# Four sums of squares in a two-block transformer kernel, regrouped between VectorE and TensorE

## The reference

```
# block 1
h = rmsnorm(x, attn_pre_g)                        # norm n0
mix = concat(nsa_attention, swa_attention) @ w_o
x = x + rmsnorm(mix, attn_post_g)                 # norm y1 -> x1
h = rmsnorm(x, mlp_pre_g)                         # norm x1
a, u = split(h @ w_gate_up)
y = (gelu(causal_dwconv(a)) * u) @ w_down
x = x + rmsnorm(y, mlp_post_g)                    # norm y2 -> x2
x = x + (p @ w_ple) * sigmoid(x @ w_ple_gate)     # -> x3
# block 2
h = rms_norm(x, norm_mix)                         # norm x3
x = x + concat(neighbourhood, retention) @ w_out  # -> x4
h = rms_norm(x, norm_mlp)                         # norm x4
x = x + square(relu(h @ w_up)) @ w_down           # -> x5
return rms_norm(x, norm_final)                    # norm x5

def rmsnorm(x, g): return x * rsqrt(mean(x * x, axis=-1) + 1e-6) * g
```

## Time and profile before

| | us |
|---|---|
| median of 3 runs | 1358.34 (1356.01 to 1365.15) |
| the profiled execution | 1356.79 |
| its span, first to last instruction | 1355.0 |

### The profile page before, as it was taken

One profiled execution on the slowest core, in us unless ns is written; L12 is line 12 of the kernel. 1 busy time (PEld: TensorE's weight loads), 2 busy tenths in 40 slices (PEclk: granted clock), 3 DMA queues, 4 the chain that ended last, 5 costly groups with the idle time before them and its releaser, 6 DMA issues.

```text
span 1355.0 us, 16819 instructions
## 1 busy us (share of the span) xinstructions
PE 1309.6 (97%) x6196; PEld 1086.0 (80%) x6196; DVE 808.7 (60%) x1562; ACT 640.3 (47%) x1234; POOL 149.8 (11%) x133
## 2 busy tenths in 40 slices
PE   8999999989999999999989999999999999999996
PEld 7897888878888888888767867788878888888885
DVE  5779989565664556445567877578553333344343
ACT  6777666454444444234344654576453233242342
POOL 0012111000110011001001100022221011020110
PEclk9989999989999999999979999999999999999998
DMA  7211010322232332323322221332223233232321
GB/s 259 83 40 47 32 32 24 131 70 78 94 93 86 109 101 86 102 93 101 93 63 78 84 74 53 93 125 90 76 73 114 94 94 101 86 108 94 95 78 62
DMA packets 63008, 118.20 MB, mean 87 GB/s; under 512 B 7632, under 2 KB 9040, under 8 KB 62672
## 3 DMA queue, kind: packets, MB, share of 16 engines
q1 hardware_dynamic: 61776, 113.48, 26.4%
q10 hardware_dynamic: 1152, 3.67, 0.8%
HBM read 115.02 MB, written 2.10 MB: 86 GB/s over the span
## 4 chain that ended last, share of the span: by engine, by line
PE 80%; DVE 12%; ACT 5%; issue 3%; DMA 1%; SPq 0%; POOL 0%; DVEq 0%; ACTq 0%
PE bank L529 23%; PE bank L531 23%; PE bank L530 23%; PE bank L586 1%; PE bank L588 1%; PE bank L587 1%; DVE pp L1866 1%; PE bank L698 1%; PE bank L615 1%; DVE wl L1695 1%; DVE ptl L1889 1%; DVE pp L1883 1%; ACT wh L1099 1%; PE bank L684 1%; PE bank L685 1%
## 5 line engine op out<-in xcount | busy, mean ns | idle before, releaser
L1695 DVE TENSOR_TENSOR wl<-raw,wh 128x512 fp32r<-128x512 f32 (+1 forms) x356 | 269.5, 772 | 362.7 <-ACT wh L1099 361.7
L1099 ACT ACTIVATE wh<-raw 128x512 fp32r<-128x512 f32 (+1 forms) x394 | 239.8, 623 | 299.0 <-PE bank L531 287.0
L529 PE MATMUL bank<-AH,wh 128*128 128x512 f32 x840 | 333.1, 397 | 8.8 <-DVE AL L1709 3.7
L531 PE MATMUL bank<-AH,wl 128*128 128x512 f32 x840 | 331.8, 395 | 0.0
L530 PE MATMUL bank<-AL,wh 128*128 128x512 f32 x840 | 329.7, 392 | 0.0
L529 PE MATMUL bank<-BH,wh 128*128 128x512 f32 x624 | 248.8, 399 | 5.8 <-DVE wl L1695 3.7
L531 PE MATMUL bank<-BH,wl 128*128 128x512 f32 x624 | 246.6, 395 | 0.0
L530 PE MATMUL bank<-BL,wh 128*128 128x512 f32 x624 | 245.1, 393 | 0.0
L529 PEld LDWEIGHTS bank<-AH,wh 128*128 128x128 f32 x840 | 158.9, 189 | 45.8 <-issue 5.4
L530 PEld LDWEIGHTS bank<-AL,wh 128*128 128x128 f32 x840 | 158.8, 189 | 35.2 <-issue 0.2
L531 PEld LDWEIGHTS bank<-AH,wl 128*128 128x128 f32 x840 | 158.8, 189 | 34.9
(11 more groups left out here) (286 smaller groups left out, 1672.1 us busy)
## 6 DMA issues: line engine op xcount, KB each, us to landing
raw<-in_w_dn SPq DMA_DIRECT2D x108, 256.0 KB, 2.6
raw<-in_w_gu SPq DMA_DIRECT2D x88, 256.0 KB, 2.6
raw<-in_w_up SPq DMA_DIRECT2D x64, 256.0 KB, 2.6
raw<-in_w_nsa SPq DMA_DIRECT2D x16, 256.0 KB, 2.6
raw<-in_w_pg SPq DMA_DIRECT2D x16, 256.0 KB, 2.6
raw<-in_w_naq SPq DMA_DIRECT2D x16, 256.0 KB, 2.7
nbi<-in_na_bias ACTq DMA_DIRECT2D x8, 448.0 KB, 3.5
raw<-in_w_swa SPq DMA_DIRECT2D x10, 256.0 KB, 2.7
```

The costliest lines, as they stand in the source:

```text
L529: t.matmul(o, w, xh, start=start, stop=False, skip_group_check=skip)
L531: return t.matmul(o, wl, xh, start=False, stop=stop, skip_group_check=skip)
L1099: a.activation(W[i % NW].h[:, 0:n], RAW[i % NRAW][:, 0:n], ACT.Copy).then_inc(*s_wh.up(i))
L1695: v.tensor_tensor(w.l[:, 0:n], RAW[i % NRAW][:, 0:n], w.h[:, 0:n], ALU.subtract).then_inc(*s_wl.up(i))
```

## The change

- y1, y2, x5: VectorE adds the squares of the chunks 1 to 6, each behind the addition of the next result chunk. TensorE sums only the added tile and that of chunk 7: two groups of four matmuls in place of five.
- x1: the square of chunk 0 goes to `r2_bc`, VectorE adds those of the chunks 1 to 7, and TensorE does one group of four, behind the first gate/up product, in place of eight groups.
- Each of these matmuls has 64 columns of ones in place of one, so a block's sum stands 64 times in the bank, and the first of each 64 is read.
- ScalarE takes the root from PSUM with the mean's factor and eps inside the instruction; before its wait it does a root of one column (`warm`), whose result nothing reads. VectorE's instruction for the mean is gone; the Newton step is rearranged, with four instructions behind the root in both kernels.
- The back product is four matmuls of 128 columns, each behind its own diagonal tile.
- In the first gate/up product the 12 matmuls of chunk 0 are ordered so that the eight that need only `AH` come first (`fresh`).
- The last half of the last product is done one result chunk at a time (`G=1, kpp=4`, with the weights packed to suit), and the loading and splitting of the last pieces is placed between the steps of the norm.

```diff
+                    if fresh is not None and s == 0:
+                        x = src[ks[0]]
+                        e.wait_ge(s_xh.at((fresh, ks[0])))
+                        for g in range(G):
+                            t.matmul(bs[g][:, :], w.h[:, g * P:g * P + P], x.h, start=True, stop=False)
+                        for g in range(G):
+                            t.matmul(bs[g][:, :], w.l[:, g * P:g * P + P], x.h, start=False, stop=False)
+                        e.wait_ge(ready(ks[0]))
+                        for g in range(G):
+                            m = t.matmul(bs[g][:, :], w.h[:, g * P:g * P + P], x.l, start=False, stop=False)
+                        m.then_inc(*s_mm.up(("p", i)))
+                        continue
...
-            def squares_of(key, c, src, first, last):
+            def squares_of(key, src, first, last, *done):
 
                 b = bank.ap(("st", key))
                 for i in range(4):
-                    m = t.matmul(b[:, i:i + 1], src[:, P * i:P * i + P], ones[:, 0:1], start=first and i == 0, stop=last and i == 3, skip_group_check=True)
-                m.then_inc(*s_st.up((key, "c", c), *([key] if last else [])))
-
-            def soon(key):
+                    m = t.matmul(b[:, 64 * i:64 * i + 64], src[:, P * i:P * i + P], ones[:, 0:64], start=first and i == 0, stop=last and i == 3,
+                                 skip_group_check=True)
+                m.then_inc(*s_st.up(*done, *([key] if last else [])))
+
+            def soon(key, alone=True):
 
                 b, free = bank.take(("st", key))
-                e.wait_ge(*free, s_ad.at((key, 3)))
-                squares_of(key, 3, r2_bc, True, False)
-                for c in range(4, 8):
-                    e.wait_ge(s_sq.at((key, c)))
-                    squares_of(key, c, sqr.ap((key, c)), False, c == 7)
+                e.wait_ge(*free, s_ad.at((key, 6 if alone else 7)))
+                squares_of(key, r2_bc, True, not alone)
+                if alone:
+                    e.wait_ge(s_sq.at((key, 7)))
+                    squares_of(key, sqr.ap((key, 7)), False, True, (key, "c", 7))
                 bank.give(("st", key))
 
             def soon_back(key):
                 b, free = bank.take(("bk", key))
-                e.wait_ge(*free, s_rs.at((key, "diag")))
-                t.matmul(b[:, :], ones[:, :], tmp.ap((key, "d"))[:, 0:T], start=True, stop=True).then_inc(*s_st.up(("bk", key)))
+                e.wait_ge(*free)
+                for i in range(4):
+                    c = slice(P * i, P * i + P)
+                    e.wait_ge(s_rs.at((key, "diag", i)))
+                    m = t.matmul(b[:, c], ones[:, :], tmp.ap((key, "d"))[:, c], start=True, stop=True)
+                m.then_inc(*s_st.up(("bk", key)))
...
-            def x1_squares(c):
-                if c == 0:
-                    b, free = bank.take(("st", "x1"))
-                    e.wait_ge(*free)
-                e.wait_ge(s_sq.at(("x1", c)))
-                squares_of("x1", c, sqr.ap(("x1", c)), c == 0, c == 7)
-                if c == 7:
-                    bank.give(("st", "x1"))
-
             c0, g0 = 0, 0
             for gi, n in enumerate(FF1):
                 for c in range(c0, c0 + n, 2):
                     keys = [("a", c), ("u", c), ("a", c + 1), ("u", c + 1)]
-                    between = None
-                    if c == 0:
-                        between = {k: lambda k=k: x1_squares(k - 1) for k in range(1, 8)}
-                    elif c == 2:
-                        x1_squares(7)
+                    if c == 2:
+                        soon("x1", False)
                         embedded(2)
                         soon_back("x1")
-                    product("w_gu", g0, A, x1, range(8), 4, 1, keys, between)
+                    product("w_gu", g0, A, x1, range(8), 4, 1, keys, fresh="x1" if c == 0 else None)
...
+                    if gi == 3 and i:
+                        for g in range(4):
+                            product("w_dn2", 56 + 2 * g, A, up_ready, range(8), 1, 4, [keys[g]])
+                            bank.give(keys[g])
+                        continue
...
-                e.wait_ge(s_rs.at((key, "var")))
-                a.activation(rv[:, 4:8], rv[:, 0:4], ACT.Sqrt).then_inc(*s_fn.up((key, "sqrt")))
+                b = bank.ap(("st", key))[:, 0:256].rearrange("p (b q) -> p b q", q=64)[:, :, 0]
+                a.activation(warm[key], eps, ACT.Sqrt)
+                e.wait_ge(s_st.at(key))
+                a.activation(rv[:, 4:8], b, ACT.Sqrt, bias=eps, scale=1.0 / 1024).then_inc(*s_fn.up((key, "sqrt")))
...
-                b = bank.ap(("st", key))
-                e.wait_ge(s_st.at(key))
-                v.tensor_scalar(rv[:, 0:4], b[:, 0:4], 1.0 / 1024, EPS, ALU.mult, ALU.add).then_inc(*s_rs.up((key, "var")))
-                bank.read(("st", key), (s_rs, (key, "var")))
+                b = bank.ap(("st", key))[:, 0:256].rearrange("p (b q) -> p b q", q=64)[:, :, 0]
+                g, h = rv[:, 4:8], rv[:, 0:4]
                 e.wait_ge(s_fn.at((key, "sqrt")))
-                v.reciprocal(rv[:, 4:8], rv[:, 4:8]).then_inc(*s_rs.up((key, 1)))
+                v.reciprocal(g, g).then_inc(*s_rs.up((key, 0)))
+                e.wait_ge(s_rs.at((key, 0)))
+                v.scalar_tensor_tensor(out=h, in0=b, scalar=1024 * EPS, in1=g, op0=ALU.add, op1=ALU.mult).then_inc(*s_rs.up((key, 1)))
+                bank.read(("st", key), (s_rs, (key, 1)))
                 e.wait_ge(s_rs.at((key, 1)))
-                v.scalar_tensor_tensor(out=rv[:, 0:4], in0=rv[:, 0:4], scalar=-0.5, in1=rv[:, 4:8], op0=ALU.mult,
-                                       op1=ALU.mult).then_inc(*s_rs.up((key, 2)))
+                v.scalar_tensor_tensor(out=h, in0=h, scalar=-0.5 / 1024, in1=g, op0=ALU.mult, op1=ALU.mult).then_inc(*s_rs.up((key, 2)))
                 e.wait_ge(s_rs.at((key, 2)))
-                v.tensor_tensor(rv[:, 0:4], rv[:, 0:4], rv[:, 4:8], ALU.mult).then_inc(*s_rs.up((key, 3)))
-                e.wait_ge(s_rs.at((key, 3)))
-                v.scalar_tensor_tensor(out=rv_out, in0=rv[:, 0:4], scalar=1.5, in1=rv[:, 4:8], op0=ALU.add,
-                                       op1=ALU.mult).then_inc(*s_rs.up((key, 4)))
+                v.scalar_tensor_tensor(out=rv_out, in0=h, scalar=1.5, in1=g, op0=ALU.add, op1=ALU.mult).then_inc(*s_rs.up((key, 4)))
                 d = tmp.ap((key, "d"))
                 e.wait_ge(s_rs.at((key, 4)), *tmp.before((key, "d")), s_tab.at("tab"))
                 for i in range(4):
-                    m = v.tensor_scalar(d[:, P * i:P * i + P], ident[:, :], rv_out[:, i:i + 1], None, ALU.mult)
-                m.then_inc(*s_rs.up((key, "diag")))
+                    v.tensor_scalar(d[:, P * i:P * i + P], ident[:, :], rv_out[:, i:i + 1], None,
+                                    ALU.mult).then_inc(*s_rs.up((key, "diag", i)))
                 tmp.read((key, "d"), (s_st, ("bk", key)))
...
-            def add_square(key, c, dst):
-                if 0 < c < 4:
+            def add_square(key, c):
+
+                if c:
                     e.wait_ge(s_sq.at((key, c)), s_sq.at((key, 0)), *([s_ad.at((key, c - 1))] if c > 1 else []))
-                    v.tensor_tensor(dst[:, :], dst[:, :], sqr.ap((key, c))[:, 0:T], ALU.add).then_inc(*s_ad.up((key, c)))
+                    v.tensor_tensor(r2_bc[:, :], r2_bc[:, :], sqr.ap((key, c))[:, 0:T], ALU.add).then_inc(*s_ad.up((key, c)))
...
+                    add_square("x1", c - 1)
+            add_square("x1", 7)
...
-    r["w_dn2"] = np.concatenate([packed(dn[1024 * i:1024 * (i + 1)], four, 1, 4) for i in range(4)])
+    r["w_dn2"] = np.concatenate([packed(dn[1024 * i:1024 * (i + 1)], four, 1, 4) for i in range(3)]
+                                + [packed(dn[3072:], four[:1], 1, 4), packed(dn[3072:], one[4:], 4, 1)])
```

32 lines of the change are left out of this document (21 added, 11 removed).

## The result

The changed kernel took 1338.35 us, the median of 4 runs (1336.99 to 1338.97), and the kernel before beside it 1357.17 (1355.43 to 1365.15). The ratio is 0.985, with a 95% interval of 0.981 to 0.989: faster by 1.5%. The forecast was 1341.0 in a range from 1335.5 to 1348.0. A second series gave 1337.28 (4 runs, 1334.26 to 1341.52) against 1356.92 (13 runs), a ratio of 0.986 (0.980 to 0.993).

What follows compares the result with a forecast made beforehand. TensorE was taken as the bound, busy for 97% of the span with 80% of the chain. Gains of 3.2 + 6.7 + 3.6 + 3.5 = 17.0 us from 1356.79 gave 1339.8, stated as 1341, range 1335.5 to 1348.

Steps and rivals of the forecast that it cites:

- y1: Norm before x1: shorter squares and an earlier root gain 3.2 us; 3.4 with full clock, 2.0 if it falls.
- x1: Stage from VectorE's first x1 instruction to the end of the squares: 34.5 to 27.8 us, 6.7 gained.
- y2: Norm before x2: earlier root and four-part back product start x2 at 680.4, not 684.02, 3.6 us gained.
- the end: Final norm, x5: root 2.0 us earlier plus a shorter back product, 3.5 us gained, from 2.5 to 4.
- the same loss: Start of the x2 stage: half clock as before, 0.50 until 691.7, then 0.89, so nothing gained there.
- no longer waits for a table: Root at y1: starts at about 282.8, 2.4 us earlier than before, without waiting for the table load.
- the last `AL` sets the end, so I give them nothing: Reordered first 12 matmuls of x1: no gain; without the cover of the last `AL`, under 1 us.
- the four-part back product saves 1.5 more: Back product at x5: split in four, it saves 1.5 us beyond the root's 2.0.
- Three terms: Gains at y1, y2 and x5, assuming a 1.28 us table load; with the drain each some 1.4 us smaller.
- The squares hold VectorE: Rival for x1: VectorE waits about 0.7 us per turn for ScalarE, turn 3.97, total 1344.5; chance 0.13.
- The clock holds at half: Rival for x1 and x2: TensorE's pauses keep the clock at 1.2 GHz, total 1376; chance 0.04.
- The wide products do not help: Rival: clock falls behind y1's squares, back products stay slow, columns cost 0.06 us a record; 1345, chance 0.15.

Runs made afterwards that it cites:

- again: The changed kernel, unaltered, profiled once more: 1339.71 us.
- before_wide: The kernel before with only its products of squares widened from one column to 64: 1358.18 us against 1355.83, one run of each.
- one_column: The changed kernel with products of squares of one column instead of 64: 1346.90 us, ratio to before 0.990.
- both: The changed kernel with x1's square additions on GpSimd and, at the end, chunk 6's addition and the table load earlier, the last scaling behind the root: 1343.49 us.
- more_vector: The changed kernel with one more VectorE pass of 128x512 in the turns of chunks 2 to 5 of x1: 1340.36 us.
- x1_on_pe: The changed kernel with x1's squares summed on TensorE chunk by chunk again, still with 64 columns: 1346.56 us, ratio to before 0.990.
- no_fresh: The changed kernel with the first 12 gate/up matmuls of x1 in the old order, waiting for `AL`: 1343.89 us.
- again_timed: The changed kernel, unaltered, timed and profiled beside the other experiments: 1337.28 us.
- no_warm: The changed kernel without the one-column warm root ahead of the real one: 1347.60 us.
- pool_adds: The changed kernel with x1's additions of squares on GpSimd instead of VectorE: 1343.11 us.

## Why the prediction was right, and where not

**The four terms.** y1 gained 3.77 (I said 3.2), x1 6.71 (6.7), y2 3.66 (3.6), the end 2.96 (3.5): 17.1 where the sum was 17.0. That the sum fits to 0.1 is in part luck, since y1 was 0.6 too low and the end 0.5 too high, and y2's term holds only with a full clock in its back product. The rest of the 18.4 us is a balance: 3.1 gained between x2 and the end, of which 1.6 to 1.8 repeat (`again`), and 1.8 lost ahead of y1, a stretch that wanders from run to run. The start of x2 is one of the gains, with a granted clock of 0.89 in 675.3 to 690.0 (0.88 and 0.86 in the other two profiles), where in the kernel before the same 14.7 us, from 687.4 on, had 0.79, and in `before_wide` 0.79 too. I had assumed the same loss there. What in the change brings it stays open: `one_column` and `both` had 0.81 and 0.80.

**y1: the term was under-sized.** The squares were through 0.4 us earlier than I had them (4.95 us behind `embedded(0)`'s first matmul, predicted 5.34), mainly because VectorE's first result addition came 1.86 us ahead of that matmul (276.62) and not 1.18 as before. `embedded(1)` took 2.85 for 2.74, and the stage came out at 8.89 for 9.24. The 3.2 was a hedge between 3.4 with the clock kept and 2.0 with it lost. It was kept, and `one_column` shows that the 64 columns kept it. The sentence that the root "no longer waits for a table" was wrong, and my own sum beside it had the root behind the load: it follows load and warm root at once, in the cover of `embedded(1)`.

**x1: right to 0.01, by a sum in which one step was wrong.** Its steps can be followed in the trace: `AL` of chunk 6 is done 21.2 us into the stage (predicted 21.3), the last chunk's products end at 27.0 (26.8), the squares at 27.8 (27.8). The fifth pass makes VectorE the bound (3.26 us, predicted 3.27), shown by `more_vector`; the wait of before was TensorE's doing, shown by `x1_on_pe`. The step "the last `AL` sets the end, so I give them nothing", on the reordered first 12 matmuls, failed. `no_fresh` puts them at 1.8 us. It holds only while TensorE keeps up, and I had reckoned with no half clock at the start of the stage. So the term was met because the edit that I gave nothing took away a loss that I had not seen: the two cancel, and that is luck.

**y2: right, where the clock held.** From the end of the squares (667.92 + 0.92, by the step of such groups) to x2 it is 2.9 us, as forecast, with the root behind them at once. But I had priced the back product at full clock. It had it in two of the three profiles of this kernel. In `again_timed` it took 2.04 us, and the gain was 2.7.

**x5: over-sized by 0.5.** The root came 3.53 us behind the last result addition, not 5.71: 2.2 earlier, for the 2.0 of the step. But "the four-part back product saves 1.5 more" was 0.8. I had priced it at full clock, and it ran at 0.57 and took 1.81 us (2.04 in `again`). `both` shows the 1.13 that I had meant.

**The rivals.** *The squares hold VectorE* didn't occur: VectorE has no wait in its turn. *The clock holds at half* didn't either: with pauses of 0.26 us per chunk the granted clock is back at 0.90 by 292 to 296. With pauses of 0.84 (`more_vector`) it was 1.00 from 287 to 300, and the stage paid for the passes and nothing more. (The "12 us over before" of this rival doesn't follow from the terms it names: 41 and 2.4 against 34.5 give 8.9.) The rule that stood behind this rival, of the Trainium skill, "TensorE: Matmul & The Clock Gate", section "A second HAM failure mode: psum-queue depth-cycling", on short pauses between groups, shows no price here at either length. *The wide products do not help* was the opposite of what happened at y1, where the clock held and the columns cost 0.03 us a group (0.92 against 0.89). Its second part was right for the end, whose back product stayed slow in all three profiles. My expectation of `one_column` repeated it in another form, that the width is worth nothing anywhere, and that fell too. Three terms rested on a table load without the drain of about 1.38 us that the Trainium skill, "ScalarE: Activation LUTs", section "What ACT_TABLE_LOAD costs", adds to it. The traces decide for them: the next activation follows the load within 0.02 us (283.08 + 1.28 and 284.38 in `no_warm`).

## What to carry to other kernels

Of a norm's sum of squares only what stands behind the last chunk needs the fastest engine, so let the engine with slack add the rest while the chunks come, and count the turn of the engine that gets the work: its new length is the new pace of the stage. Price short serial stretches at both clock levels, and give TensorE whatever it can start early, since the half-clock stretch is cheap when it falls on a time with little to do. Read small gains by stages between two named instructions: here they repeat to 0.01 us at y1 and x1, where whole times wander by 10. Look at what ended such a stage before calling a cause: in `before_wide` the clock was kept, and yet half of the gain was lost to a root that came late.

## What the runs showed of the hardware

Products of 64 columns and of 1 column take nearly the same time, 0.115 and 0.111 us per record (0.92 and 0.89 us for eight), but the granted clock behind them was 1.00 in one case and 0.62 in the other. A table load starts ahead of the wait of the activation that needs it: in `no_warm` it ran from 1332.36 to 1333.65 and the squares' last record only started at 1333.37. A VectorE addition of two SBUF tiles beside a GpSimd pass took 1.25 us instead of 0.69, and a weight remainder 1.78 (`pool_adds`). And dense products ran 2% slower in some runs at a granted clock of 1.00, which no experiment here explains.
